# Second block of a two-block transformer on one core: pass-by-pass order in the channel-major projections and in one gate unit, and the order of ScalarE's and VectorE's steps in the attention's tail

## The reference, cut to what matters

```python
for i in range(DEPTH_2):                                 # two layers
    hn = rms_norm_2(h, attn_norm[i])
    proj = hn @ w_in[i]
    (c_q, c_kv, k_rope, dq, dk, dv, iq, ik, iw, sq, sk, sv) = jnp.split(proj, offsets, axis=-1)
    q  = (rms_norm_2(c_q, mla_q_norm[i]) @ mla_w_uq[i])   # latent heads: 6
    kv = (rms_norm_2(c_kv, mla_kv_norm[i]) @ mla_w_ukv[i])
    ...
    # latent: softmax(q k^T) v
    # sparse: scores from iq, ik, iw choose the 64 best keys of each query; softmax over these of dq dk^T + bias
    # stick: w = exp(log_sigmoid(z) + suffix sums of log_sigmoid(-z)), z = sq sk^T
    h = h + mix @ w_o[i]                                  # mix: the three groups of heads side by side
    hf = rms_norm_2(h, ffn_norm[i])
    h = h + (jax.nn.silu(hf @ w_gate[i]) * (hf @ w_up[i])) @ w_down[i]
    g = jax.nn.sigmoid(rms_norm_2(h, ple_norm[i]) @ w_ple_gate[i])
    h = h + g * (p[i] @ w_ple_proj[i])
return rms_norm_2(h, final_norm)
```

## Time and profile before

| | us |
|---|---|
| median of 3 runs | 997.58 (997.21 to 997.60) |
| the profiled execution, its own time | 997.25 |
| its span (first to last instruction) | 995.1 |
| outside of the span | 2.15 |
| TensorE busy in the span | 968.7 (97%) |
| VectorE / ScalarE / GpSimd busy | 625.8 / 504.0 / 30.6 |
| mean granted TensorE clock | 0.998 |

### The profile page before, as it was taken

How to read it: one execution, slowest core, us unless ns; L and a number is a source line. 1 busy time by engine, 2 the same in 40 slices (tenths; PEclk the granted TensorE clock), 3 DMA queues, 4 the chain that set the end, 5 groups by cost and what they waited for, 6 DMA issues and landing times.

```text
span 995.1 us, 13296 instructions
## 1 busy us (share of the span) xinstructions
PE 968.7 (97%) x5508; PEld 824.0 (83%) x5508; DVE 625.8 (63%) x771; ACT 504.0 (51%) x637; POOL 30.6 (3%) x49
## 2 busy tenths in 40 slices
PE   7999899999999999999999999999999999999996
PEld 5766699999988998788888888899987788888885
DVE  5899765554468398765454546763996655554565
ACT  4556655444465456554444445644575543434453
POOL 1000000000002000010000000010000100000010
PEclk9999999999999999999999999999999999999999
DMA  9998848665424532446555555454505454545521
GB/s 341 400 419 328 328 166 348 247 259 208 166 98 152 191 130 84 164 164 211 189 192 180 201 173 199 145 189 154 184 30 201 169 211 172 202 177 190 191 106 43
DMA packets 31222, 196.60 MB, mean 198 GB/s; under 512 B 3891, under 2 KB 5992, under 8 KB 10168
## 3 DMA queue, kind: packets, MB, share of 16 engines
q1 hardware_dynamic: 31162, 195.75, 53.5%
HBM read 194.67 MB, written 2.05 MB: 198 GB/s over the span
## 4 chain that ended last, share of the span: by engine, by line
PE 80%; DVE 11%; DMA 3%; issue 3%; ACT 2%; POOL 0%; SPq 0%; DVEq 0%; POOLq 0%; ACTq 0%
PE ps L1805 57%; PE ps L2167 8%; PE ps L2254 5%; DVE lo L1171 2%; DMA raw<-stream 1%; DMA scratch<-stream 1%; ACT hi L676 1%; PE ps L2508 1%; PE ps L2390 1%; PE ps L2195 1%; DVE scratch L1603 1%; PE ps L1891 1%; DVE raw L1241 1%; PE ps L2281 1%; DVE scratch L1663 1%
## 5 line engine op out<-in xcount | busy, mean ns | idle before, releaser
L1171 DVE TENSOR_TENSOR lo<-raw,hi 128x2048 fp32r<-128x2048 f32 (+6 forms) x139 | 303.4, 2186 | 210.8 <-ACT hi L676 210.7
L676 ACT ACTIVATE hi<-raw 128x2048 fp32r<-128x2048 f32 (+4 forms) x139 | 259.4, 1869 | 125.3 <-PE ps L1805 100.8
L1805 PE MATMUL ps<-hi,xh 128*128 128x512 f32 (+3 forms) x676 | 265.5, 393 | 6.0 <-DVE xl L1467 3.2
L1805 PE MATMUL ps<-lo,xh 128*128 128x512 f32 (+3 forms) x676 | 261.4, 387 | 0.0
L1805 PE MATMUL ps<-hi,xl 128*128 128x512 f32 (+3 forms) x676 | 261.0, 386 | 0.0
L1805 PEld LDWEIGHTS ps<-hi,xh 128*128 128x128 f32 x676 | 126.9, 188 | 35.7 <-issue 7.1
L1805 PEld LDWEIGHTS ps<-lo,xh 128*128 128x128 f32 x676 | 126.9, 188 | 25.5
L1805 PEld LDWEIGHTS ps<-hi,xl 128*128 128x128 f32 x676 | 127.1, 188 | 23.5
L1805 PE MATMUL ps<-hi,gh 128*128 128x512 f32 (+2 forms) x308 | 118.4, 385 | 0.0
L1805 PE MATMUL ps<-lo,gh 128*128 128x512 f32 (+2 forms) x308 | 118.1, 383 | 0.0
L1805 PE MATMUL ps<-hi,gl 128*128 128x512 f32 (+2 forms) x308 | 118.1, 383 | 0.0
(11 more groups left out here) (298 smaller groups left out, 1183.9 us busy)
## 6 DMA issues: line engine op xcount, KB each, us to landing
raw<-stream SPq DMA_DIRECT2D x140, 1024.0 KB, 4.8
scratch<-stream SPq DMA_DIRECT2D x22, 1024.0 KB, 9.6
raw<-stream SPq DMA_DIRECT2D x4, 1020.0 KB, 4.8
raw<-stream SPq DMA_DIRECT2D x4, 896.0 KB, 4.7
raw<-stream SPq DMA_DIRECT2D x2, 864.0 KB, 4.4
raw<-stream SPq DMA_DIRECT2D x2, 768.0 KB, 4.6
raw<-stream SPq DMA_DIRECT2D x2, 680.0 KB, 3.9
h<-x SPq DMA_DIRECT2D x2, 512.0 KB, 5.1
```

What stands on the lines that cost most here:

```text
L676: nc.scalar.activation(hi[:, u["s"] % SPLIT_SLOTS, first:n], raw_of(u, n)[:, first:n], ACT.Copy).then_inc(S["hi_done"], 1)
L1171: nc.vector.tensor_tensor(lo[:, slot, first:n], raw_of(u, n)[:, first:n], hi[:, slot, first:n].bitcast(F32), ALU.subtract).then_inc(S["lo_ ...
L1805: ins = nc.tensor.matmul(out, l, r, start=start and i == 0, stop=stop and i == 2, skip_group_check=skip)
```

## The change

In `channel_unit` the three passes are no longer side by side: for each piece of a unit, first all high x high, then all with the rows' low part, then all with the weights' low part, and only ahead of the last pass the wait for `lo`. The first pass waits for `hi_done`. The same is done for part 1 of the first `gu` pair at the first block of tokens (`low_last`). On ScalarE, the two copies go ahead of the dummy Softplus, and the `hi` of `wo`'s second unit behind the two Softplus. On VectorE, the copy of the second transposes goes ahead of three rounds of the search, and the first sparse norm ahead of the `lo` of `wo`'s second unit.

```diff
@@ ScalarE
                 spare = slice(4 * layer + 3, 4 * layer + 4)
-                nc.scalar.activation(half_var[:, spare], pow_half[:, 0:1], ACT.Softplus)
                 product(act, ("sb", layer))
                 nc.scalar.activation(sT[:, 0:2, :], ..., ACT.Copy, scale=DH ** -0.5).then_inc(S["sb_evac"], 1)
                 nc.scalar.activation(sT[:, 2:4, :], ..., ACT.Copy).then_inc(S["sb_evac"], 1)
-                feed(last_of(("sb", layer)))
+                nc.scalar.activation(half_var[:, spare], pow_half[:, 0:1], ACT.Softplus)
                 for g, (heads, banks) in enumerate(SB_GROUPS):
                     ...
                     nc.scalar.activation(sbt[:, heads, :], ps[:, banks, 0:3 * P], ACT.Softplus).then_inc(S["s_sp"], 1)
+                feed(last_of(("sb", layer)))
@@ VectorE
                 nc.vector.tensor_copy(pmT[1], ...).then_inc(S["m_pT"], 1)
-                top_keys(5, 6)
                 dve.wait_ge(S["m_pT_ps"], 2 * layer + 2)
                 nc.vector.tensor_copy(pmT[0], ...).then_inc(S["m_pT"], 1)
-                top_keys(6, TOPK // 8)
+                top_keys(5, TOPK // 8)
...
                 mix_low(1)
+                sparse_norm(0, 1)
                 feed(last_of(("wo", layer)), -2)
-                sparse_norm(0, 1)
                 sparse_norm(1, 0)
@@ TensorE, token_major (low_last=(1,) for the first gu pair)
+                            if by_pass:
+                                pe.wait_ge(S["hi_done"], u["s"] + 1)
+                                for i, (a, w) in enumerate(((ah, wh), (al, wh), (ah, wl))):
+                                    if w is wl:
+                                        parts(u)
+                                    for k in range(u["kts"]):
+                                        if w is wl:
+                                            rest_of(u, k)
+                                        ...one matmul for each column range
@@ TensorE, channel_unit
-                    wh, wl = parts(u)
-                    for cs4, k in ((cs4, k) for cs4 in pieces for k in range(u["kts"])):
-                        ...
-                        for c in cs4:
-                            for i, (a, w) in enumerate(((xh, wh), (xl, wh), (xh, wl))):
-                                ins = nc.tensor.matmul(...)
+                    wh, wl = views(u)
+                    pe.wait_ge(S["hi_done"], u["s"] + 1)
+                    for cs4 in pieces:
+                        ...
+                        for i, (a, w) in enumerate(((xh, wh), (xl, wh), (xh, wl))):
+                            if w is wl:
+                                parts(u)
+                            for k in range(u["kts"]):
+                                if w is wl:
+                                    rest_of(u, k)
+                                for c in cs4:
+                                    ins = nc.tensor.matmul(...)
```

More of the change, by code:

```diff
@@ L1792, in parts, with views @@
                         lo[:, s, 0:n].rearrange("p (k c) -> p k c", k=u["kts"]))
+            def views(u):
+                n, s = u["kts"] * u["cols"], u["s"] % SPLIT_SLOTS
+                return tuple(w[:, s, 0:n].rearrange("p (k c) -> p k c", k=u["kts"]) for w in (hi, lo))
             def rest_of(u, k):
@@ L1807, in three, with token_major @@
                 return ins
-            def token_major(units, ah, al, columns, place, done=None, opened=False, waits=None, closed=True, together=(), between=None):
+            def token_major(units, ah, al, columns, place, done=None, opened=False, waits=None, closed=True, together=(), between=None, low_last=()):
                 sizes, groups, at = list(together) or [1] * len(units), [], 0
@@ L1822, in token_major @@
                                 between(u, b)
+                            by_pass = b == 0 and u["part"] in low_last
                             if b == 0:
-                                weights[u["s"]] = parts(u)
+                                weights[u["s"]] = views(u) if by_pass else parts(u)
                             wh, wl = weights[u["s"]]
@@ L1828, in token_major @@
                             sl = slice(b * P, (b + 1) * P)
-                            for k in range(u["kts"]):
+                            if by_pass:
[6 more added lines that the diff above has]
+                                            rest_of(u, k)
+                                        kk = u["k0"] + k
+                                        for at, c in enumerate(columns):
+                                            ins = nc.tensor.matmul(place(b, at), a[:, kk, sl], w[:, k, c], start=kk == 0 and i == 0 and not opened,
+                                                                   stop=closed and i == 2 and u is units[-1] and k == u["kts"] - 1)
+                            for k in range(0 if by_pass else u["kts"]):
                                 kk = u["k0"] + k
@@ L2565, in _ @@
                                 done=lambda ins: ins.then_inc(S["gu_ps"], 1), waits=waits, together=(2,) if j < 2 else (),
-                                between=(second_T, first_hidden, None)[min(j, 2)])
+                                between=(second_T, first_hidden, None)[min(j, 2)], low_last=(1,) if j == 0 else ())
                     if j == 1:
```

14 lines of the change are left out of this document (6 added, 8 removed).

## The result

| | before | after |
|---|---|---|
| median of 6 runs each, same chip | 997.39 us (996.75 to 997.87) | 991.23 us (990.73 to 991.99) |
| ratio, 95% interval | | 0.9936 (0.9926 to 0.9945) |
| profiled execution, its span | 997.25, 995.1 | 991.57, 989.4 |
| chain that ended last: TensorE, VectorE | 80%, 11% | 88%, 5% |

What follows compares the result with a forecast made beforehand. TensorE was taken as the bound (80% of the chain of waits), so only its gaps count. Per layer 1.43 + 0.88 + 0.75 = 3.06, for both 6.12, from 997.25 to 991.13; median put at 991.2, range 989.8 to 994.0.

Steps and rivals of the forecast that it cites:

- `dsa` units: TensorE's `dsa` matmuls in attention: passes apart remove gaps of 0.18 and 0.50 and a 0.10 restart, 0.78 us a layer.
- stick logits: Tail, TensorE: with ScalarE's copies ahead of the dummy Softplus, these logits start 1.14 us earlier.
- VectorE's first copy: Tail, ahead of the second group of logits: this copy comes only 0.5 us earlier, ending at 385.52.
- second group of logits: Tail, TensorE: writes the banks VectorE's first copy reads, so starts 0.84 us earlier; 0.3 of the 1.14 is lost.
- sparse logits: Tail, TensorE: the wait for VectorE's second copy, 0.59 us in starts, goes; with 0.84 they come 1.43 earlier.
- sparse norm's gap: TensorE ahead of the sparse weights' transposes: the 0.88 us wait for the norm standing behind a `lo` goes entirely.
- `gu` pair: Feed-forward, second unit of the first pair: the wait for the second piece of `lo` and its restart go, 0.75 us.
- order of passes, added waits: 600 reordered matmuls, bounded at 0 to 1.2 us, and added waits, at most 1.1 us in all; both taken as 0.
- `lo` becomes the wait: Rival at `wo`'s second unit: cover is only 0.3; if late, up to 0.88 a layer returns, 992.9 us; chance 0.10.
- VectorE keeps the tail: Rival: latent norms 0.5 later than thought, so a layer gives 2.1, 993.0 us; chance 0.12.
- The drain of the table load: Rival at ScalarE's Exp: the skill's 1.38 us per table switch delays the sparse logits some 0.5 a layer, 992.1; chance 0.03.
- Slower, passes dearer: Rival: passes apart load each weight tile anew; 0.014 us on 600 matmuls adds 8.4, giving 999.5; chance 0.03.

Runs made afterwards that it cites:

- only_act: Kernel before with ScalarE's new order alone (copies ahead of the dummy Softplus, `hi` behind the Softplus): 997.49 us, ratio 0.9998.
- no_copy: Changed kernel with VectorE's second latent copy behind a round of the search again: 992.36 us, ratio to before 0.9950.
- hi_early: Changed kernel with the `hi` of `wo`'s second unit straight behind the two copies, ahead of the dummy and both Softplus: 990.77 us, ratio to before 0.9938.
- no_act: Changed kernel with ScalarE in the old order (dummy Softplus ahead of the copies, `hi` ahead of the Softplus): 993.09 us, ratio to before 0.9961.
- after_again: The changed kernel itself once more, run beside warm_mid on the same chip: 991.62 us, ratio to before 0.9941.
- warm_mid: Changed kernel with six extra 128x128 matmuls on constants in TensorE's wait before the first MLP product: 990.92 us, ratio to before 0.9934.
- only_copy: Kernel before with VectorE's second copy straight behind the first, ahead of the search rounds, alone: 996.54 us, ratio 0.9992.

## Why the prediction was right, step by step

The mechanism of each step was right, and several terms were mis-sized by up to 0.2, in both directions.

| step, per layer | forecast | measured |
|---|---|---|
| `dsa` units | 0.78 | 0.70 |
| stick logits | 1.14 | 0.99 |
| VectorE's first copy | 0.5 | 0.58 |
| second group of logits | 0.84 | 0.90 |
| of the stick logits' shift, lost at the first copy | 0.3 | 0.09 |
| sparse logits | 1.43 | 1.43 |
| sparse norm's gap | 0.88 | 0.88 |
| `gu` pair | 0.75 | 0.75 |
| order of passes, added waits | 0 | 0 (0.120 a matmul in both) |
| sum | 3.06 | 3.06 |

- **`dsa`, mis-sized by 0.08.** The term of 0.18 for unit 0 is where it failed. Its restart behind the 16 records still takes longer than the 0.1 that I put from the drawn length of the last one; only 0.09 went. The 0.60 of unit 1 was right.
- **Stick logits, mis-sized by 0.15.** Besides these 0.08, the gap ahead of them was put too large. The text says near 0.39 in starts, while the 1.14 has 1.70 - 1.34 = 0.36 in it. The 12 transposes fill 1.40 up to the next start (383.32 - 381.92), where I had left 1.34, and the gap was 1.70 - 1.40 = 0.30.
- **Why that did not matter.** The second group waits for the later of two, and that is VectorE's first copy: TensorE's 0.99 is cut to 0.90 there. The misses ahead of it fell within the 0.3 that the forecast took off there, so only 0.09 had to be lost. VectorE gained 0.58, not 0.5, and the sparse logits 0.53 on top, not 0.59; these two errors of 0.06 cancel, and that the tail comes to 1.43 to the hundredth is luck.
- **The hand-overs.** The one at VectorE's second copy is shown by two experiments: 0.28 won and given back in only_act, and 0.90 cut to 0.59 in no_copy. The one at its first copy has no experiment of its own. For it speak the distances from the stick logits to the second group: 2.60 or 2.61 in eight of the kernels of the table, and 2.69 or 2.70 in after, no_copy and hi_early, where the stick logits are 0.99 early, with a start 0.06 behind the copy's end in after.
- **Covers.** For the Exp 0.4 was put and 0.41 measured; for the `lo` of `wo` 0.3, and 0.29 measured. The rival that `lo` becomes the wait did not come; `lo` would have had to be 0.29 later.
- **VectorE keeps the tail.** Half true: it sets the second group. But its norms of the latent weights ended at 381.72, 0.20 ahead of the transposes (shift 0.70, no wait), so the 2.1 a layer of that rival was not what came.
- **The drain of the table load.** A load of 1.28 and an instruction 0.01 behind it, at the switch to Softplus (383.22, then 384.51); at that to Exp the load follows the `hi` at once (389.91, then 389.93), is over at 391.21, and the Exp starts at 391.62. The page ScalarE: Activation LUTs of the Trainium skill, section What ACT_TABLE_LOAD costs, adds 1.38 a switch; this trace does not agree.
- **Slower, passes dearer.** This rival needed 0.010 a matmul or more. The pieces of 96 take 11.51 in both orders, equal to 0.01 us in all.
- **The median.** 997.25 - 6.12 = 991.13; the profiled execution took 991.57, as 0.52 was lost ahead of the first stretch, at the clock. The forecast names the 0.33 by which the median of before stood above its profiled execution, but with it the sum would be 991.46 and not 991.2. Median and forecast are 0.03 apart, closer than the working or the runs (1.3 us wide) can bear out: that is luck, and what is shown is the 3.06 a layer.

## What to carry to other kernels

Where one engine is the bound, read its gaps as distances between starts, and follow each one through every hand-over behind it before you add it to the sum: a shift passes a hand-over only as far as the later partner has moved. A part that gives nothing alone (ScalarE's order here) can be worth 0.62 a layer with the others, so leave-one-out and one-alone tests answer different questions, and both are needed. Putting the passes that need the late operand last cost nothing here in TensorE's order and took the wait away. Look first for such an order, and for a copy that stands behind a table load or a search.

## What the runs showed of the hardware that was not expected

Executions of one kernel differ by 1 us and more: the kernel before took 996.61 to 1001.01 in 33 runs. The profiles part in two places, both ahead of the changed stretch. By the start of the first product of the MLP, at 112 us, they already stand up to 1.3 us apart (112.08 in no_copy, 113.41 in no_act); the expectation for after_again, that executions differ only by the clock, leaves this out. From 112 to 124 us, behind that start, TensorE's granted clock is not the same from profile to profile. The rows are that window's, with its length, the busy time of TensorE, its weight loads, VectorE, ScalarE and GpSimd with counts, the granted clock, the DMA share and GB/s. In the kernel after:

```profile
112.00:124.00 12.00, 10.91 (x44) 8.63 (x45) 7.42 (x17) 8.97 (x20) 0.55 (x1) 0.86 0.78 300
```

In hi_early:

```profile
112.00:124.00 12.00, 10.32 (x47) 8.06 (x48) 7.68 (x17) 9.56 (x21) 0.55 (x1) 1.00 0.75 296
```

Of the 13 profiles seven show 1.00 (before, only_act and warm_mid among them), four 0.86 and two 0.72 (only_copy and no_act), and the parts of the change all lie behind it in the program. In the timeline of after, TensorE comes out of a wait of about 2 us there:

```profile
112.58 0.70 PE L1809 MATMUL ps<-hi,xh 128*128 128x512 f32 x1 [1.93 <-DVE xl L1467]
113.08 0.63 PE L1809 MATMUL ps<-hi,xl 128*128 128x512 f32 x1
113.50 0.63 PE L1809 MATMUL ps<-lo,xh 128*128 128x512 f32 x1
...
116.29 0.39 PE L1809 MATMUL ps<-hi,xh 128*128 128x512 f32 x1
116.52 0.40 PE L1809 MATMUL ps<-hi,xl 128*128 128x512 f32 x1
```

The matmuls stand 0.43 apart (512 columns at 1.2 GHz) and later 0.23 (2.4 GHz). In hi_early the same wait has no such sequel:

```profile
112.40 0.47 PE L1809 MATMUL ps<-hi,xh 128*128 128x512 f32 x1 [1.92 <-DVE xl L1467]
```

The wait is 1.92 or 1.93 in all profiles but that of warm_mid, so its length does not decide whether the clock falls. With the wait filled, in warm_mid:

```profile
112.24 0.47 PE L1809 MATMUL ps<-hi,xh 128*128 128x512 f32 x1 [0.58 <-DVE xl L1467]
112.54 0.40 PE L1809 MATMUL ps<-hi,xl 128*128 128x512 f32 x1
```

they are at the higher level at once, and the window shows 1.00. But six profiles without the filling show that too, so one profile does not prove that the filling did it, and its effect on the median stays open. What a fall costs can be read from the distance between the start of this product and that of the changed stretch (237.90 in after, 350.48 - 112.58). It is 237.35 to 237.40 in the seven profiles at 1.00, warm_mid's 237.35 among them, 237.78 to 238.22 in the four at 0.86, and 240.07 and 240.09 in the two at 0.72. So a fall of the clock in an untouched stage moved the changed stretch by 0.4 to 0.8 or by 2.7 us, the latter more than any one part of this change is worth in both layers. The 0.52 between before and after is of the first kind.
